# Two transformer blocks on one Trainium2 core: the q/k panels of the last attention in seven-chunk steps, on two banks, with its end and a weight split of the gated mixer in new order

## The reference

```python
# gMLP mixer: out = (u * (W_s v + b)) W_out, then swiglu, then
k, v = shared_kv(x, kv_norm, kv_w)          # 8 heads, 2 x 64 key columns, 128 value columns
q = (rms_norm(x, b_norm) @ b_w_q)           # 8 heads, 2 x 64 query columns
for head, block of 128 queries:             # 8 x 4 = 32 items
    s = q k^T * scale - slope * distance    # two score matrices per head, causal
    p = softmax(s)
    a = p[0] - lam * p[1]
    o[head] = a @ v
o = rms_norm(o of each head, subln) * (1 - lambda_init)
x = x + o @ b_w_o
```

## Time and profile before

| what | value |
|---|---|
| median of three runs | 1892.91 us |
| profiled execution, its own time | 1893.12 us |
| its span, first to last instruction | 1891.3 us |
| TensorE busy in it | 1861.0 us, 98% |
| DVE, ACT, POOL busy | 1097.0, 768.1, 257.8 us |
| time that lies around the span | 1.8 us |
| items 0 to 37 and the columns behind them | 1323.98 to 1489.72 us |

### The profile page before, as it was taken

How to read it: one execution, slowest core, us unless ns; L and a number is a source line. 1 busy time by engine, 2 the same in 40 slices (tenths; PEclk the granted TensorE clock), 3 DMA queues, 4 the chain that set the end, 5 groups by cost and what they waited for, 6 DMA issues and landing times.

```text
span 1891.3 us, 24875 instructions
## 1 busy us (share of the span) xinstructions
PE 1861.0 (98%) x8756; PEld 1524.8 (81%) x8756; DVE 1097.0 (58%) x1575; ACT 768.1 (41%) x1181; POOL 257.8 (14%) x206
## 2 busy tenths in 40 slices
PE   7999999999999999999999999999999999999998
PEld 6877888788888888887888888888787888888886
DVE  5867976777677624676544442254888654444323
ACT  4226664355545413563422322143557433323212
POOL 4702320020000001301100000021643110000001
PEclk9999999999999999999999999999998999999998
DMA  4232332122222332222223223332111223222232
GB/s 174 96 105 74 101 101 78 56 90 92 96 100 89 122 100 89 91 88 89 89 100 100 89 100 100 99 100 97 66 62 34 67 91 99 99 94 96 99 100 78
DMA packets 62837, 174.48 MB, mean 92 GB/s; under 512 B 5428, under 2 KB 23988, under 8 KB 62648
## 3 DMA queue, kind: packets, MB, share of 16 engines
q1 hardware_dynamic: 61424, 169.50, 27.1%
q10 hardware_dynamic: 1016, 2.92, 0.5%
q0 software_dynamic: 336, 1.25, 0.2%
HBM read 171.54 MB, written 2.10 MB: 92 GB/s over the span
## 4 chain that ended last, share of the span: by engine, by line
PE 90%; DVE 5%; ACT 1%; issue 1%; POOL 1%; DMA 1%; SPq 0%; POOLq 0%; DVEq 0%; ACTq 0%
PE ps L472 29%; PE ps L474 28%; PE ps L473 28%; PE ps L999 1%; DVE w_lo L1670 1%; POOL square_sum L2448 1%; DMA w_raw<-in_weights 1%; PE ps L1010 1%; ACT w_hi L1108 0%; PE ps L954 0%; DVE at_e L1898 0%; PE ps L492 0%; DVE sg_z L2195 0%; DVE sg_t L2191 0%; PE ps L667 0%
## 5 line engine op out<-in xcount | busy, mean ns | idle before, releaser
L1670 DVE TENSOR_TENSOR w_lo<-w_raw,w_hi 128x1024 fp32r<-128x1024 f32 x315 | 405.5, 1288 | 461.5 <-ACT w_hi L1108 461.1
L472 PE MATMUL ps<-xg_hi,w_hi 128*128 128x512 f32 (+1 forms) x1448 | 566.0, 391 | 11.5 <-DVE w_lo L1670 10.0
L473 PE MATMUL ps<-xg_lo,w_hi 128*128 128x512 f32 (+1 forms) x1448 | 559.0, 386 | 0.0
L474 PE MATMUL ps<-xg_hi,w_lo 128*128 128x512 f32 (+1 forms) x1448 | 558.6, 386 | 0.0
L1108 ACT ACTIVATE w_hi<-w_raw 128x1024 fp32r<-128x1024 f32 x315 | 331.6, 1053 | 540.1 <-PE ps L474 534.6
L472 PEld LDWEIGHTS ps<-xg_hi,w_hi 128*128 128x128 f32 x1448 | 273.7, 189 | 76.9 <-DVE w_lo L1670 16.7
L474 PEld LDWEIGHTS ps<-xg_hi,w_lo 128*128 128x128 f32 x1448 | 273.6, 189 | 54.9
L473 PEld LDWEIGHTS ps<-xg_lo,w_hi 128*128 128x128 f32 x1448 | 273.9, 189 | 53.5 <-issue 1.0
L472 PE MATMUL ps<-hid_hi,w_hi 128*128 (+1 forms) x528 | 205.5, 389 | 0.0
L474 PE MATMUL ps<-hid_hi,w_lo 128*128 (+1 forms) x528 | 205.4, 389 | 0.0
L473 PE MATMUL ps<-hid_lo,w_hi 128*128 (+1 forms) x528 | 205.4, 389 | 0.0
(11 more groups left out here) (368 smaller groups left out, 2445.9 us busy)
## 6 DMA issues: line engine op xcount, KB each, us to landing
w_raw<-in_weights SPq DMA_DIRECT2D x315, 512.0 KB, 3.3
out_cols<-result SPq DMA_DIRECT2D x8, 256.0 KB, 2.2
x<-in_x_cols SPq DMA_DIRECT2D x2, 512.0 KB, 5.8
x<-in_x_cols SPq DMA_DIRECT2D x1, 1024.0 KB, 9.0
squares<-in_mem_cols ACTq DMA_DIRECT2D x1, 512.0 KB, 3.8
sp_w<-in_spatial ACTq DMA_DIRECT2D x1, 512.0 KB, 4.3
sp_b<-in_spatial_bias ACTq DMA_DIRECT2D x1, 512.0 KB, 5.1
dil<-in_dil_table POOLq DMA_DIRECT2D x1, 448.0 KB, 9.2
```

What stands on the lines that cost most here:

```text
L472: nc.tensor.matmul(to, wh, xh, start=start, stop=False)
L473: nc.tensor.matmul(to, wh, xl, start=False, stop=False)
L474: return nc.tensor.matmul(to, wl, xh, start=False, stop=stop)
L1670: nc.vector.tensor_tensor(w_lo[:, u % 2, :], w_raw[:, u % 2, :], w_hi[:, u % 2, :].bitcast(F32), ALU.subtract).then_inc(w_ready, 1)
```

## The change

Seven things change. The names are those of the code.

1. `SLOWER = (7, 11, 15, 19)`: in these items three chunks of a panel are done, not four. Every later chunk stands one, two, three and then four chunks further on, and the last four stand in item 26. A panel that ended with an odd item now ends with the first chunk of item 8 and 10, the second of 12 and 14, the third of 16 and 18, the fourth of 20, 22, 24 and 26.
2. Panels go to banks 7 and 3 in turn, and the first chunk of a panel waits for the panel before the last to be read, not for the last.
3. From item 8 on DVE does `panel_out` behind `least(n)`, ahead of `probs(n-3)`; before, it was the first thing of the item.
4. Spreads: heads 0 and 1 behind the panel chunks of item 26, heads 2 and 3 in item 27 (before: 26, 27, 27, 28), on other banks; `head_normed`, `head_hi` and `head_lo` follow them.
5. Sums of heads 4, 5 and 6 in items 29, 32, 36 (before 28, 32, 36), and they wait for the four normed heads.
6. Output columns 0 to 3 in items 29, 30, 31, 33 (before 30, 31, 33, 35), with the weight splits that follow them.
7. In the gated mixer DVE splits unit 2 of `a_out` ahead of the eight scalings of x, not behind them.

```diff
+SLOWER = (7, 11, 15, 19)
...
+    def panel_chunks(n):
+        def done(m):
+            return min(KC // 2 * m - sum(s < m for s in SLOWER), KC * (2 * N_DIFF - EARLY_PANELS))
+        return range(done(n), done(n + 1))
+
+    def panel_bank(p):
+        return 7 if p % 2 else 3
...
-        COLUMN_ITEMS = (BO_EARLY, BO_EARLY + 1, BO_EARLY + 3, BO_EARLY + 5)
+        COLUMN_ITEMS = (BO_EARLY - 1, BO_EARLY, BO_EARLY + 1, BO_EARLY + 3)
+        LATER_SUMS = (29, 32, 36)
...
# TensorE, diff_item
                 if n == 25:
+                    pe.wait_ge(kv["qk"], 2 * N_DIFF - 1)
                     heads_turned(0, 3)
+                if n == 27:
+                    pe.wait_ge(kv["qk"], 2 * N_DIFF)
+                    head_spread(2, 7)
+                    pe.wait_ge(a3["normed"], 1)
+                    head_spread(3, 2)
+                if n in LATER_SUMS:
+                    pe.wait_ge(a3["normed"], 4)
+                    head_sums(4 + LATER_SUMS.index(n))
+                for g in panel_chunks(n):
+                    p, k = EARLY_PANELS + g // KC, g % KC
+                    if k == 0:
+                        pe.wait_ge(w_ready, qk0 + p + 1)
+                        if p >= EARLY_PANELS + 2:
+                            pe.wait_ge(kv["qk"], p - 1)
...
                 if n == 26:
+                    head_spread(0, 2)
                     head_spread(1, 3)
-                p = EARLY_PANELS + n // 2
-                if p < 2 * N_DIFF:
-                    if n % 2 == 0 and n:
-                        pe.wait_ge(kv["qk"], p)
-                    half_panel(qk0 + p, ps[:, 7, :], *qk_input(p), n % 2)
...
# DVE
+            split(FIRST["a_out"] + 2)
             for c in range(KC):
                 nc.vector.scalar_tensor_tensor(out=x[:, c, :], ...)
...
-                if panel_due(n):
-                    panel_out(EARLY_PANELS - 1 + n // 2, 7)
+                p = EARLY_PANELS - 1 + n // 2
+                if panel_due(n) and n < SLOWER[0]:
+                    panel_out(p, panel_bank(p))
                 if live(n - 5):
                     lo(n - 5)
                 if live(n - 2):
                     inverse(n - 2)
                 if live(n):
                     least(n)
+                if panel_due(n) and n > SLOWER[0]:
+                    panel_out(p, panel_bank(p))
                 if live(n - 3):
                     probs(n - 3)
+                if n == 26:
+                    head_normed(0, 2)
+                    head_normed(1, 3)
...
                 if n == 27:
-                    head_normed(1, 3)
                     head_normed(2, 7)
+                    head_normed(3, 2)
                     head_lo(0)
+                    head_lo(1)
```

More of the change, by code:

```diff
@@ L978, in output_column @@
                     pe.wait_ge(a3["out_lo"], 4)
-                if j < 2:
-                    pe.wait_ge(a3["normed"], 3 + j)
-                else:
+                if j >= 2:
                     pe.wait_ge(early["added"], ADDED["bo_early"] + j - 1)
@@ L1033, in diff_item @@
                     scores(n)
-                if n >= 12 and n % TB == 0 and n // TB - 3 < N_DIFF - 1:
+                if n >= 12 and n % TB == 0 and n // TB - 3 < 4:
                     head_sums(n // TB - 3)
                 if n == 25:
+                    pe.wait_ge(kv["qk"], 2 * N_DIFF - 1)
                     heads_turned(0, 3)
+                if n == 27:
[12 more added lines that the diff above has]
+                            pe.wait_ge(kv["qk"], p - 1)
+                    wh, wl = tile((qk0 + p) % 2, k)
+                    hi, lo = qk_input(p)
+                    mm = product(ps[:, panel_bank(p), :], wh, wl, hi[:, k, :], lo[:, k, :], k == 0, k == KC - 1)
+                    if k == KC - 1:
+                        mm.then_inc(used, 1)
                 if n == 26:
-                    pe.wait_ge(kv["qk"], 2 * N_DIFF)
-                    head_spread(0, 7)
-                if n == 27:
+                    head_spread(0, 2)
                     head_spread(1, 3)
[L1043 to L1047, removed]
-                p = EARLY_PANELS + n // 2
-                if p < 2 * N_DIFF:
-                    if n % 2 == 0 and n:
-                        pe.wait_ge(kv["qk"], p)
-                    half_panel(qk0 + p, ps[:, 7, :], *qk_input(p), n % 2)
                 if n in COLUMN_ITEMS:
@@ L1613, in diff_item @@
                     head_hi(0)
+                    head_hi(1)
                 if n == 28:
-                    head_hi(1)
                     head_hi(2)
-                if n == 29:
                     head_hi(3)
@@ L1704, in into_residual @@
                 elif n > LAST:
-                    split(u0 + 2)
+                    if not done:
+                        split(u0 + 2)
                     split(u0 + 3)
@@ L2239, in _ @@
             dve.wait_ge(x_ready, KC * NORM["a"])
-            into_residual("a_out", KC, "ffn0", "ffn_norm0", 0)
+            into_residual("a_out", KC, "ffn0", "ffn_norm0", 0, 1)
             def swiglu(name, norm, base):
@@ L2357, in diff_item @@
                     heads_lo(0)
-                if n == 26:
-                    head_normed(0, 7)
                 if n == 27:
-                    head_normed(1, 3)
                     head_normed(2, 7)
+                    head_normed(3, 2)
                     head_lo(0)
+                    head_lo(1)
                 if n == 28:
-                    head_normed(3, 3)
-                    head_lo(1)
                     head_lo(2)
-                if n == 29:
                     head_lo(3)
```

## The result

| | before | changed |
|---|---|---|
| time, median | 1892.91 us (1891.71 to 1893.11) | 1905.31 us (1904.83 to 1905.68) |
| span of the profiled execution | 1891.3 us | 1903.8 us |

A forecast was written before the change was run, and what follows sets the result against it. TensorE, busy 1861.0 of 1891.3 us, was taken to bound the kernel. Terms -1.7 - 0.2 - 2.7 + 6.1 + 1.5 + 3.6 - 2.1 + 3.0 = +7.5 us gave 1900.5 us, range 1893.5 to 1906.5 (eight in ten).

The forecast's parts named there:

- the signs that the prediction named: Some 12 us of turn waits in 7 to 10, two over 2 us; own heads_turned wait; attention some 9 us longer.
- `a_out` split: In a_out, the 1.58 us w_lo wait and the slow first product behind it go: -1.7 us.
- second bank: In the panels, one can start before the last one is read: -0.2 us.
- chunks that leave items 7 to 25: Four chunks of three products leave these items and come back in item 26: -2.7 us there.
- new waits of turns, items 14 to 24: TensorE waits for panel_out and probs behind the panel's end, 0.25 us in item 14 to 1.61 in 22: +6.1 us.
- `heads_turned`, item 25: Its chain starts with ACT's split, which now waits for the panel's end: wait of 1.5 us, bounds 0.5 and 2.
- items 26 to 29 with their waits, full clock: 14.6 us of work plus waits of 0.7, 2.3 and 3.6 make 21.2 us against 17.61 before: +3.6 us.
- items 30 to 37: One output column less, -2.85 us, against 0.7 us of waits it had covered: -2.1 us.
- clock, up to item 29: One fall of 1.5 us in item 25 and 1.5 of unhidden half clock in item 29: +3.0, between 0 and 8.
- the rival in which the order doesn't bind: Items 14 to 25: DVE finishes panel and probabilities while TensorE has work, so no waits; -6 us, 1887; chance 0.08.
- The premise on the clock: In item 27 of the kernel before, the level was said to fall after 1.78 us of waiting and thin work.
- The rival with the clock at full: Whole change without the clock term, since waits of 1.58 us in a_out's dense work leave it full: +4.5, 1897.5; chance 0.20.

The follow-up runs named there:

- the one with the probabilities first: Changed kernel with probs(n-3) ahead of panel_out on DVE from item 8 on, still behind least(n): 1901.28 us, ratio 1.0042.
- With filling: Changed kernel with 2, 3 and 5 unused products (6.8 us in all) ahead of the turns of items 21, 24 and 25: 1903.16 us, ratio 1.0053.
- The kernel of the last run: Kernel before with the a_out split, item 26's probabilities ahead of the minima, and head_normed(0, 7) ahead of that item's w_lo: 1888.57 us, ratio 0.9977.

## Why the prediction was right, and where it was too small

The sign and the mechanism held: the panel's end, now ahead of a `turn`, puts DVE's read and the probabilities on TensorE's path. Of the signs that the prediction named, `turn` waits in nine pieces, which grow up to item 22, but 9.9 us and not 12, with one wait over 2 us and not two; `heads_turned` has its own wait; and items 0 to 37 take 15.3 us longer (1321.45 to 1489.72, before 1323.98 to 1476.96), not some 9. The total stays in the range, 1.2 us below its upper end, in part by luck: the waits came out 3.2 us shorter than forecast (5.0 and 4.5 for 6.1 and 6.6), against a clock and an end that cost more. By its terms (the profiled executions, cut at the same instructions):

| term | forecast | measured |
|---|---|---|
| `a_out` split | -1.7 | -1.7 (item 0 starts 2.5 sooner, 0.8 of it from the wait at the kernel's start); -2.2 by its own run |
| second bank | -0.2 | nothing measurable (the kernel with two banks and the old end stands 0.3 above the split alone) |
| chunks that leave items 7 to 25 | -2.7 | in the -0.8 up to item 20, which also holds 1.25 of waits: -2.1 without them |
| new waits of turns, items 14 to 24 | +6.1 | +5.0 in five waits: 0.49, 0.76, 1.17, 1.44, 1.18 |
| `heads_turned`, item 25 | +1.5 | +1.52 |
| items 26 to 29 with their waits, full clock | +3.6 (waits 6.6) | waits 4.5; the 2.1 less is set against the clock below |
| items 30 to 37 | -2.1 | +0.3 |
| clock, up to item 29 | +3.0 | about +6.3 (1.7 and 4.6) |

*The panels.* The chain from the last product's end was right to 0.01: 1.17 us for two blocks and 1.44 for four, and 1.17, 1.44 and 1.18 were measured behind items 20, 22 and 24. The 0.17 that I had added for the overlap isn't in these, since the profile counts a wait from the last product's end, so the lost overlap shows as busy time instead. It fits what the windows have too much: items 20 to 25 are busy 2.35 us longer than before, 1.7 by the clock and 0.65 over, for four waits. The same 0.17 is all that the waits behind items 16 and 18 fall short of the forecast (0.49 and 0.76 for 0.66 and 0.93), and most of what item 14 does (none for 0.25); by the run with two shifted chunks a turn doesn't wait while the panel ends with the second chunk or before. DVE was indeed idle for the panel (1.80 us), and the rival in which the order doesn't bind is out.

I had set a rule of the Trainium skill aside here ("SBUF — State Buffer", section "Who interferes with whom"). The trace bears out the choice: the probabilities took 0.74 at 1422.03 although POOL's queue was started by the panel's read, and it is the `w_lo` behind them that takes 2.06 us against 1.23 for the same instruction in `a_out`. In item 26 that `w_lo` (2.16 us) is in the chain to `turn(24)`, whose 6.1 to 7.2 us allowed for it (7.3 measured, from 1447.04 to 1454.35). POOL does slow other probabilities: those of 384 columns took 2.09 us at 1415.02, beside POOL's head bias, and 0.62 at 1461.35 with POOL idle. No turn waits behind them in the changed kernel; in the one with the probabilities first they take 2.08 at 1415.07, and that turn is the one that waits 1.10.

*The step that was mis-sized is the clock.* The prediction took "one fall of 1.5 in item 25 and 1.5 of unhidden half clock in item 29". The first measured 1.7 (5.00 us at a mean of 0.66, 1436 to 1441). The second was 17 us at a mean of 0.51. Items 26 to 29 then have 21.3 us of busy time where their work at full clock was put at 14.6: 6.7 us more, of which 2.1 came back as shorter waits (4.5 against 6.6), so 4.6 unhidden in place of 1.5. (The 14.6 is an estimate; the window from 1450 to 1467, 12.83 us busy at 0.51, gives some 6.3 us lost to the clock by itself.) Why more than I thought: I put the half clock in item 29, and it began in item 27, at 1450.4, ahead of both long waits; and I let the half clock end with the waits, but it goes on through output column 0, which the new order puts right behind them. The column ran its 12 products in 5.27 us (1461.92 to 1467.19) in place of 2.85. That is 2.4 of the 3.1 us that were missing. With filling the half clock was 3.4 us long and the column ran at full clock, so that the half clock costs is shown; that it comes from the long waits is not, and that the column under it costs 2.4 us is read from the trace, not tried by itself.

*Items 30 to 37* had to bring 2.1 and brought nothing. There were 1.58 us of waits, not 0.7 (`turn(29)` 0.31, the sums of head 6 for ACT's squares 0.96, a weighing 0.31), and another half clock began at 1488, some 0.9. Some 0.7 us more is busy time that neither explains; the three waits at the 0.17 above would make 0.5 of it, which is an estimate.

*What the terms had mixed up.* The runs divide the 12.4 us by parts instead of places: split -2.2, banks and late read +0.3, new end +5.8, two shifted chunks +1.8, two more +6.6 (12.3). The prediction never said what the new end costs by itself. Alone it only loses: three turns wait 4.6 us with nothing shifted at all, where the old end has one wait of 1.8; in the order on DVE two divisions stand ahead of the `w_lo` of item 26 and two more, with two `head_lo`, behind the next probabilities. I had seen that queue, but charged it to the late panels. No run separates the order of the divisions from the new places of columns and sums.

*The premise on the clock was wrong.* "The level fell after 1.78 us of waiting and thin work": the wait isn't needed. The kernel of the last run has none there, and falls at 1441.1; and the changed kernel falls at 1450.4 with 0.32 us of waiting in the 4 us ahead. The rival with the clock at full was never near, and for another reason than the one given against it.

## What to carry to other kernels

Where a long-running accumulation ends right ahead of an instruction that waits for another engine, and that engine reads the accumulation first, count the chain from the last product on; here it cost nothing while two chunks (1.36 us) stood behind the end, 0.5 to 0.8 us with one chunk there and 1.2 to 1.4 with none, so try a shift at half its size. Test an order of several parts part by part: here the one that gained (2 us) was hidden beneath two that lost. Ask which engine idles where another waits: one line, the probabilities ahead of the minima in the one item where DVE had 1.2 us to spare, brought another 1.9 us and gave 1888.8 us, below both kernels (0.9977 of before, interval [0.9968, 0.9986]).

## What the runs showed of the hardware that I had not expected

- TensorE's clock fell from 2.4 to 1.2 GHz with no wait ahead of it: busy 2.90 of 2.91 us at 1.00, then 0.53 over 11 us. What stood there was transposes, scores on 64 rows, spreads on four rows and the start of a weighing. It also held over waits: 1.53 us at 1432.8 with two chunks shifted, where the changed kernel fell behind a wait of the same length 2.5 us after another of 1.18; and over 1.44 us in item 23 of the changed kernel, where with filling elsewhere a wait of 1.53 at the same place was followed, 1.6 us on, by 3.2 us at 0.53. So waiting time alone doesn't foretell it.
- Once low, it stays low for 3.2 to 4 us in dense work, and for 10 to 17 us where thin work and waits go on. In the kernel with filling it fell amid 15 dense matmul instructions, at 1459.2, some 1.0 us after they had begun behind a wait of 2.2 us, and was back at 1462.7.
- The idle stretch ahead of a wait's end isn't all that it costs: the first four transposes behind a wait took 0.66 us against 0.60 in a stream.
